# Another pace for the scattered gate cells of a PEER encoder block

## What is computed

```
q  = x @ w_q                                 # per head two halves
v1, i1 = top_k(q[...,0] @ k1.T, 16);  v2, i2 = top_k(q[...,1] @ k2.T, 16)
top_s, pos = top_k(v1[:,None] + v2[None,:], 16)
idx = (i1 * 128 + i2) at pos;  g = softmax(top_s)
y   = sum over the 8*16 picks of g * gelu(x . u_tab[idx]) * v_tab[idx]
out = layer_norm(alpha * x + y)
```

## Time and profile before

| | us |
|---|---|
| median of 3 runs | 1562.07 (1558.25 to 1562.52) |
| span of the profiled execution | 1558.7 |
| PE busy in it | 1500.1 (96%) |
| DVE busy | 1227.6 (79%) |
| ACT busy | 767.2 (49%) |
| POOL busy | 687.5 (44%) |

### The profile page before, as it was taken

The page is one execution under the profiler, slowest core; times in us unless marked ns, Lnnn a source line. Parts: engine busy times, 40 slices in busy tenths (PEclk is TensorE's granted clock), DMA queues, the critical chain, the costliest instruction groups (busy, mean ns, idle before and its releaser), DMA issues.

```text
span 1558.7 us, 20955 instructions
## 1 busy us (share of the span) xinstructions
PE 1500.1 (96%) x7484; PEld 1313.8 (84%) x7484; DVE 1227.6 (79%) x2144; ACT 767.2 (49%) x1427; POOL 687.5 (44%) x400
## 2 busy tenths in 40 slices
PE   6999989999998989999999899999999999999996
PEld 5877747799998988999999788888888888888885
DVE  7569987587999957977775488887888878898885
ACT  3559990323324456877773444444444433444442
POOL 4843244474468677887688032222222221211100
PEclk9999999999999999999999999999999999999999
DMA  7527310333334768999999998989999889999971
GB/s 272 176 88 238 120 38 7 122 129 121 110 88 137 248 202 259 283 257 298 280 305 339 362 372 330 359 337 356 338 352 344 328 328 379 381 391 392 387 264 70
DMA packets 150982, 396.98 MB, mean 255 GB/s; under 512 B 29408, under 2 KB 70752, under 8 KB 134496
## 3 DMA queue, kind: packets, MB, share of 16 engines
q1 hardware_dynamic: 87520, 246.58, 43.1%
q0 software_dynamic: 36864, 134.30, 26.4%
q10 hardware_dynamic: 26496, 14.78, 3.3%
HBM read 349.40 MB, written 46.20 MB: 254 GB/s over the span
## 4 chain that ended last, share of the span: by engine, by line
PE 76%; DVE 10%; POOL 4%; DMA 3%; ACT 3%; issue 3%; DVEq 0%; POOLq 0%; ACTq 0%; SPq 0%
PE bank L1817 33%; PE bank L994 26%; PE bank L826 6%; PE bank L1445 5%; PE bank L1685 3%; POOL gate_matrix L286 3%; PE bank L881 2%; DMA u_raw<-in_peer_u_turned 2%; DVE xc L723 1%; DMA gate_matrix<-gate_values,gate_cells 1%; PE bank L1433 1%; POOL rms L526 1%; DVE hit_late L1077 1%; POOL gathered L1158 1%; DMA gathered<-in_peer_rows,expert_rows 1%
## 5 line engine op out<-in xcount | busy, mean ns | idle before, releaser
L1158 POOL DMA_INDIRECT gathered<-in_peer_rows,expert_rows x128 | 188.6, 1473 | 494.2 <-DVE gather_sum L1196 483.2
L994 PE MATMUL bank<-xhi,ut_hi 128*128 128x384 f32 x1024 | 350.6, 342 | 12.6 <-POOL ut_lo L1021 6.5
L994 PE MATMUL bank<-xhi,ut_lo 128*128 128x384 f32 x1024 | 345.0, 337 | 0.0
L994 PE MATMUL bank<-xlo,ut_hi 128*128 128x384 f32 x1024 | 344.2, 336 | 0.0
L286 POOL DMA_INDIRECT gate_matrix<-gate_values,gate_cells x128 | 249.6, 1950 | 70.4 <-issue 35.0
L1857 ACT ACTIVATE v_hi<-gate_rows_then_feed 128x1024 fp32r<-128x1024 f32 x128 | 135.7, 1061 | 225.7 <-PE bank L1817 217.2
L1817 PE MATMUL bank<-v_hi,w_hi 128*128 128x512 f32 x760 | 234.8, 390 | 2.4 <-DVE w_lo L1921 2.3
L1817 PE MATMUL bank<-v_hi,w_lo 128*128 128x512 f32 x760 | 234.4, 390 | 0.0
L1817 PE MATMUL bank<-v_lo,w_hi 128*128 128x512 f32 x760 | 234.4, 389 | 0.0
L994 PEld LDWEIGHTS bank<-xhi,ut_hi 128*128 128x128 f32 x1024 | 194.0, 189 | 17.8 <-POOL ut_lo L1021 8.6
L994 PEld LDWEIGHTS bank<-xlo,ut_hi 128*128 128x128 f32 x1024 | 193.9, 189 | 1.8
(11 more groups left out here) (250 smaller groups left out, 2386.4 us busy)
## 6 DMA issues: line engine op xcount, KB each, us to landing
u_raw<-in_peer_u_turned SPq DMA_DIRECT2D x128, 512.0 KB
gate_rows_then_feed<-in_peer_rows SPq DMA_DIRECT2D x128, 512.0 KB
gate_rows_then_feed<-gate_matrix SPq DMA_DIRECT2D x64, 384.0 KB
activations<-gel SPq DMA_DIRECT2D x48, 384.0 KB
acts_in<-activations SPq DMA_DIRECT2D x48, 384.0 KB
u_raw<-in_w_in_chunks SPq DMA_DIRECT2D x28, 512.0 KB, 4.2
gate_matrix<-gate_zeros SPq DMA_DIRECT2D x8, 1024.0 KB, 7.7
gate_rows_then_feed<-in_peer_wq_chunks SPq DMA_DIRECT2D x16, 512.0 KB, 4.5
```

The source lines that it names most:

```text
L994: ins = self.nc.tensor.matmul(self.bank[b + r % 2][:, 0:DTOK], u[r % 2][:, k, :], x[:, k, 0:DTOK], start=(i == 0), stop=(i == 3 * KD - 1))
L1158: self.nc.gpsimd.indirect_dma_start(out=self.tile[q % RING][:, :], out_offset=None, in_=self.table, in_offset=bass.IndirectOffsetOnAxis(ap ...
```

## The change

Scatters start at query step 10 and no longer at step 13: steps 10, 11 and 12 issue one each. In the gate steps s = 7 to 15 those with an odd m (and, as before, those with m a multiple of 6) issue one in place of two. All other steps issue as many as they did. The number of scatters, their cells and all other work are the same. Up to the gate step 6 three more scatters have been issued than before (19 for 16), and from step 15 on one fewer (32 for 33 behind step 15); the last one moves from step 67 to step 68.

```diff
 FIRST_GATHER = 6
+FIRST_SCATTER = 10
 
 def scatters(m):
 
-    if m < QC - 3:
+    if m < FIRST_SCATTER:
         return 0
-    if m < QC or m >= BY_QUERIES + BY_POOL:
-        return 1 if m >= QC and m % 6 == 0 else 2
-    return 1
+    if QC - 3 <= m < QC:
+        return 2
+    if m < BY_QUERIES + BY_POOL or m < BY_QUERIES + HOT_AT and m % 2:
+        return 1
+    return 1 if m % 6 == 0 else 2
```

## The result

The changed kernel takes 1568.1 us (median of 10 runs, 1564.45 to 1574.11) against 1561.85 us before (10 runs, 1558.25 to 1563.63): a ratio of 1.0041 with a 95% interval of 1.0026 to 1.0057. It is slower by 0.4%, and the forecast was 1568.6.

What follows compares the result with a forecast made beforehand. It took PE's matrix work to bound most of the kernel, with POOL's queue the chain early in the gate stage; 18.0 + 2.5 - 14 = +6.5 us on 1562.07 gave 1568.6 us, range 1561 to 1577.

Steps and rivals of the forecast that it cites:

- The stall: Query step 10: POOL's first scatter waits for DVE's list of cells, so PE's product of block 10 starts 18.0 us late.
- The short lengths: DVE's list: three instructions shorten while POOL stands, 6.2 us less in all, so the list comes at 416.6.
- The lower clock: Behind the query-stage pause PE restarts at its lower clock level, losing 2.5 us (bounds 1.5 to 3.1).
- Nothing is caught up in the query stage: PE has no slack there, so DVE's start on the last scores comes 20.5 us late (bounds 19.5 to 28).
- Gathers 5, 6 and 7: Gate stage: POOL issues them at 547, about 554.5 and 568 to 569, so DVE's three waits for tiles go.
- What comes back: Gate stage, product of step 18 to that of step 25: 14 us return (bounds 10 to 15.1).
- The sum: Whole kernel: 18.0 + 2.5 - 14 = +6.5 us, giving 1568.6 us.
- Nothing past step 25: Gate stage past step 25: tiles were already in time, so the change there is 0.
- The chances: Whole kernel: 0.64 for slower, 0.28 for within what a measurement can tell apart, 0.08 for faster.
- the list comes no earlier: Rival, query stage: DVE's long lengths are its own, +6.2 us on the sum, 1574.8 us; chance 0.08.
- less comes back: Rival, gate stage: scatter 16's landing wait or delayed expert loads leave 7 of the 14 us, 1575.6 us; chance 0.17.
- Not slower: Rival, end of gate stage: 7 us of waits for expert-block loads go too, 1559.5 us; chance 0.18.

Runs made afterwards that it cites:

- run 4: The changed kernel with its first scatter at query step 11 in place of 10: 1565.0 us.
- run 5: The changed kernel with its first scatter at query step 12 in place of 10, and two scatters in place of one at gate step 65: 1550.1 us.
- run 3: The changed kernel with its three early scatters issued in query steps 13 to 15, three each in place of two: 1549.0 us.
- run 8: run 3 with one scatter moved from gate step 20 to gate step 29: 1549.2 us.
- run 10: run 2 with one scatter more in gate step 23: 1554.2 us.
- run 2: The kernel before with only gate steps 7 to 15 at the halved pace, and two scatters in place of one at steps 53, 59 and 65: 1563.4 us.
- run 7: The kernel before with one scatter more in query step 15, gate steps 7 to 15 issuing two each as before: 1554.9 us.
- run 1: The changed kernel with its early scatters kept, but gate steps 7 to 15 at the old pace of two each: 1576.4 us.
- run 6: run 3 with gate steps 7 to 15 at the old pace of two scatters each: 1559.0 us.
- run 9: run 7 with one scatter moved from gate step 20 to gate step 29: 1555.9 us.

## Why the prediction was right

Step by step, as it was put:

- **The stall.** Forecast 18.0 us, measured 17.5 (422.56 - 403.87 - 1.16). The list came at 417.4 in this execution, so at 416.2 in the times of before, against 416.6. The short lengths were the right choice; with DVE's own lengths PE would have been 24 us late. Runs 4 and 5 show the same wait at 7.3 us and at none.
- **The lower clock.** Forecast 2.5 us (1.5 to 3.1), measured 2.2: a product of 6.41 in place of 4.19, with 0.50 granted.
- **Nothing is caught up in the query stage.** DVE starts on the last scores at 482.67, foretold near 482; at gate step 15 the offset is still 20.8.
- **Gathers 5, 6 and 7.** With the 20.8 taken off they come at 547.8, 554.4 and 568.2; the working had 547, 554.5 and 568 to 569. Gather 6 waits for DVE's addition, as it said.
- **What comes back.** Forecast 14 us, bounded by PE at 15.1; measured 14.8 between steps 15 and 24, and 14.9 between steps 18 and 25, the stretch of the bound. Runs 3, 4, 5, 8 and 10 return 14.8 or 14.9 as well, whatever they do with the scatters: the bound by PE's own work was the number to trust.
- **The sum** was +6.5, and the medians give +6.3. That they meet within 0.2 us is luck: the three terms as measured come to 17.5 + 2.2 - 14.8 = +4.9, and the interval of the ratio reaches from 4.1 to 8.9 us. The mechanism is what was right, term by term.
- **Nothing past step 25.** This term was put at 0. In the trace PE's offset goes from +6.0 to +5.1 at step 65 and to +7.2 at step 76, and 4.2 more are lost behind it, so that the span differs by +11.4 (1570.1 against 1558.7). The profiled execution is one of the slower ones of its kernel (1572.1, 4.0 above the median), which is about as much as the 4.2; in run 3, with the same gate steps, they are 1.5.
- **The chances.** A hundredth was lost in adding them: 0.40 of the forecast and the first two rivals (0.08 and 0.17) make 0.65 for slower, not 0.64.

Where the reasoning was thinner than its result: it treated the moved scatter 16 as free and the fewer scatters as what brings the tiles in time, as if they were one. Runs 2 and 7 show that either alone returns most of it (12.7 and 13.6 us by step 24). Both together are wanted for another reason, to keep it: of the pace alone nothing is left at the end. I had not seen either that the shift by three scatters also moves the later landing waits: numbers 32, 48 and 96 were second in their steps and are first now, 64 and 80 the other way round. Run 10 shows what one such shift is worth, 9 us with the halved pace.

Of the rivals, "the list comes no earlier" and "less comes back" are ruled out by the rows above. "Not slower" said that the tail of the gate stage would recover 7 us; ACT's waits for loads from 840 to 900 (total, times, longest) fell from 15.9 only to

```profile
ACT ut_hi L1007 <- DMA u_raw<-in_peer_u_turned: 12.1, 4, 6.4
```

and PE's offset goes from +5.1 at step 65 to +0.6 at step 73 and to +7.2 at step 76. So 4.5 us do come back for a few steps and are lost again: nothing of it is kept.

**What stays open.** Where scatter 112 is second in step 58 or 60 (runs 2, 4, 7 and 9), 2.9 to 10.0 us are lost between steps 65 and 70, and nothing where it is second in step 57 (runs 1 and 6). 8.1 and 3.4 us are lost behind a scatter 48 that is second in step 22 (runs 1 and 6), and nothing where it is second in steps 24 and 25 (runs 8 and 9). POOL's lead, which I counted at gather 10, doesn't explain it, but the traces show what goes with the loss: the gather that stands first behind the waiting scatter, and how long after its issue DVE asks for its tile. In run 1 that is gather 11, on POOL and its dot product on DVE:

```profile
628.23 2.07 POOL L289 DMA_INDIRECT gate_matrix<-gate_values,gate_cells  x1 [7.15 <-DMA gate_matrix<-gate_values,gate_cells]
...
637.38 1.01 POOL L1161 DMA_INDIRECT gathered<-in_peer_rows,expert_rows  x1 [0.30 <-issue]
```

```profile
643.65 1.23 DVE L1178 SCALAR_TENSOR_TENSOR gathered<-gathered,h 128x1024 f32<-128x1024 f32 x1 [6.79 <-DMA gathered<-in_peer_rows,expert_rows]
```

DVE asks for the tile at 636.9 (643.65 - 6.79), before the gather is issued. In run 9 gather 11 was put ahead of scatter 48 (by `ahead`), and behind it comes gather 12, which DVE takes 14.8 us after its issue, without a wait:

```profile
617.50 1.44 POOL L1163 DMA_INDIRECT gathered<-in_peer_rows,expert_rows  x1 [0.30 <-issue]
```

```profile
632.31 1.23 DVE L1180 SCALAR_TENSOR_TENSOR gathered<-gathered,h 128x1024 f32<-128x1024 f32 x1
```

It is the same in the other cases: the gather first behind the scatter was issued at most 6.6 us before DVE asked for its tile in all those with a loss (runs 1 and 6 behind scatter 48; runs 2, 4, 7 and 9 behind scatter 112), and 14.8 us or more before in all those without (runs 8 and 9 behind scatter 48; runs 1 and 6, with gather 27, behind scatter 112). The losses of runs 2, 4 and 10 between steps 24 and 33 belong to tiles (8, 9 and 11) whose gathers stand ahead of scatter 48. It is not the whole of it: behind scatter 112 of the changed kernel, which is first in its step, gather 29 comes 6.6 us before DVE asks for its tile, and DVE's waits there (0.92 and then 3.58 us) cost PE nothing by step 70. This is read from the traces; no run was made to vary it alone, and it does not say by how much each run loses.

## What to carry to other kernels

An instruction that is moved ahead in an in-order queue takes its wait along, and everything that stood ahead of it now stands behind that wait: find the producer's time first, and move it only as far as that (step 12 here was free, step 11 cost 9 us, step 10 cost 19). What a stage can give back is bounded by the work of the engine that is late next, and that bound, not the sum of the waits removed, was what all good versions reached. Where every n-th transfer waits for the n before it, a shift of the count by one moves all these waits, so look at where each of them falls, and at which transfer stands next behind it, before the pace itself is judged.

## What the runs showed of the hardware

- The price of PE's restart didn't grow with the pause. Behind pauses of 17.5 us the product of 24 matmuls took 6.41 (changed kernel) and 5.94 us (run 1), behind one of 7.3 us 5.93 (run 4), and 4.19 at the full clock: 1.7 to 2.2 us lost each time.
- The landing of a scatter that another one waits for directly behind it held POOL for 4.4 to 11.2 us in the rows above, while its issue takes POOL 1.5 to 3.4. With two scatters in a step, one such wait is worth two to five issues.
- With something issued in between, the wait was shorter in these traces and not always gone. In the changed kernel scatter 16 came 7.4 us behind number 15, with a multiply between them, and scatter 32 5.2 us behind number 31, with a gather between them, and POOL idled 0.16 and 0.30 us for them. But with one gather in between scatter 112 still waited 4.69 us in the same trace, and scatter 48 waited 2.94 in run 7 and 3.14 in run 10. With two gathers (scatter 48 in the changed kernel) or three (scatter 16 in run 7) it was 0.30.
